# High-part products first, and eight raw buffers for the expert tiles, in a two-layer encoder on one core

## The reference

```python
for i in range(DEPTH):                       # DEPTH = 2
    mod = c_act @ mod_w[i] + mod_b[i]
    sh_a, sc_a, g_a, sh_f, sc_f, g_f = jnp.split(mod, N_MOD, axis=-1)
    y = mixers[i % N_MIXERS](modulate(x, norm_g[i, 0], sh_a, sc_a))
    x = x + g_a[:, None, :] * rms_norm(y, norm_g[i, 1])
    y = channel_mixers[i % 2](modulate(x, norm_g[i, 2], sh_f, sc_f))
    x = x + g_f[:, None, :] * rms_norm(y, norm_g[i, 3])
```

```python
for e in range(N_EXPERTS):
    y = y + gates[..., e:e + 1] * swiglu(h, w_gate[e], w_up[e], w_down[e])
```

## Time and profile before

| | |
|---|---|
| median of 3 runs | 1932.63 us (1931.55 to 1934.05) |
| the profiled execution, own time | 1931.99 us |
| its span, first to last instruction | 1930.2 us |
| mean granted TensorE clock | 0.973 |
| busy share of TensorE, VectorE, ScalarE | 89%, 72%, 57% |
| read from HBM | 501.29 MB, 260 GB/s over the span |

### The profile page before, as it was taken

One profiled execution on the slowest core, in us unless ns is written; L12 is line 12 of the kernel. 1 busy time (PEld: TensorE's weight loads), 2 busy tenths in 40 slices (PEclk: granted clock), 3 DMA queues, 4 the chain that ended last, 5 costly groups with the idle time before them and its releaser, 6 DMA issues.

```text
span 1930.2 us, 26016 instructions
## 1 busy us (share of the span) xinstructions
PE 1727.2 (89%) x9941; PEld 1382.1 (72%) x9941; DVE 1380.4 (72%) x1236; ACT 1096.2 (57%) x1075; POOL 51.4 (3%) x100
## 2 busy tenths in 40 slices
PE   1998898899999998889888999899999988999996
PEld 1997898779999686556656676667666656778774
DVE  4557356567677487488687878786878777887885
ACT  2434433543333445477666667676757767767763
POOL 2000000001111000000000000000000000000000
PEclk9998998999999999999999999999999998999998
DMA  9865276138878330289789889898989898989993
GB/s 300 301 238 187 77 252 240 43 128 305 296 273 289 126 131 23 88 300 363 252 285 331 289 303 347 304 348 306 346 300 348 278 317 319 350 328 336 354 343 97
DMA packets 244301, 503.87 MB, mean 261 GB/s; under 512 B 10296, under 2 KB 82144, under 8 KB 244192
## 3 DMA queue, kind: packets, MB, share of 16 engines
q1 hardware_dynamic: 228688, 451.44, 66.3%
q0 software_dynamic: 13824, 50.34, 7.2%
q10 hardware_dynamic: 1680, 0.60, 0.2%
HBM read 501.29 MB, written 1.05 MB: 260 GB/s over the span
## 4 chain that ended last, share of the span: by engine, by line
PE 67%; DVE 15%; ACT 10%; issue 7%; DMA 1%; DVEq 0%; ACTq 0%; POOL 0%; POOLq 0%
PE ps L849 14%; PE ps L850 14%; PE ps L851 14%; DVE wlo L1340 7%; PE ps L1164 7%; ACT whi L544 6%; PE ps L1165 6%; PE ps L1191 4%; PE ps L1146 2%; PE ps L1235 2%; PE ps L901 1%; DMA mraw<-mod_w 1%; DVE acc L1352 1%; ACT arena L744 1%; PE ps L918 1%
## 5 line engine op out<-in xcount | busy, mean ns | idle before, releaser
L1340 DVE TENSOR_TENSOR wlo<-raw,whi 128x2048 fp32r<-128x2048 f32 x428 | 971.8, 2288 | 385.7 <-ACT whi L544 385.2
L544 ACT ACTIVATE whi<-raw 128x2048 fp32r<-128x2048 f32 x428 | 815.3, 1912 | 375.2 <-PE ps L1165 188.2
L1164 PE MATMUL ps<-whi,ahi 128*128 128x512 f32 x560 | 236.0, 421 | 48.8 <-DVE wlo L1340 42.3
L849 PE MATMUL ps<-whi,ahi 128*128 128x512 f32 (+1 forms) x688 | 244.7, 356 | 18.0 <-DVE wlo L1340 14.3
L849 PE MATMUL ps<-ahi,whi 128*128 128x256 f32 x832 | 238.3, 286 | 5.1 <-issue 2.8
L851 PE MATMUL ps<-whi,alo 128*128 128x512 f32 (+1 forms) x688 | 238.8, 347 | 0.0
L850 PE MATMUL ps<-wlo,ahi 128*128 128x512 f32 (+1 forms) x688 | 238.8, 347 | 0.0
L850 PE MATMUL ps<-alo,whi 128*128 128x256 f32 x832 | 237.3, 285 | 0.0
L851 PE MATMUL ps<-ahi,wlo 128*128 128x256 f32 x832 | 237.2, 285 | 0.0
L1165 PE MATMUL ps<-wlo,ahi 128*64 128x512 f32 x560 | 225.0, 402 | 0.0
L1164 PEld LDWEIGHTS ps<-whi,ahi 128*128 128x128 f32 x560 | 108.4, 193 | 115.5 <-issue 69.5
(11 more groups left out here) (229 smaller groups left out, 1985.6 us busy)
## 6 DMA issues: line engine op xcount, KB each, us to landing
raw<-l_exp_w_gate SPq DMA_DIRECT2D x112, 1024.0 KB, 7.0
raw<-l_exp_w_up SPq DMA_DIRECT2D x112, 1024.0 KB, 7.3
raw<-l_exp_w_down SPq DMA_DIRECT2D x112, 1024.0 KB, 6.8
mraw<-mod_w POOLq DMA_DIRECT2D x96, 512.0 KB, 5.7
raw<-l_w_in SPq DMA_DIRECT2D x42, 1024.0 KB, 5.1
raw<-l_ffn_w_gate SPq DMA_DIRECT2D x14, 1024.0 KB, 5.1
raw<-l_ffn_w_up SPq DMA_DIRECT2D x14, 1024.0 KB, 6.2
raw<-l_ffn_w_down SPq DMA_DIRECT2D x14, 1024.0 KB, 5.0
```

The source lines that it names most:

```text
L544: act.activation(whi[s % SPL][:, :], raw[s % RAW][:, :], ACT.Copy).then_inc(hi_done, 1)
L849: pe.matmul(dst, stat[0], mov[0], start=start, stop=False, skip_group_check=True)
L1164: pe.matmul(bank(b), stat, hi, start=start, stop=False, skip_group_check=True)
L1340: dve.tensor_tensor(wlo[s % SPL][:, :], raw[s % RAW][:, :], whi[s % SPL][:, :].bitcast(F32), ALU.subtract).then_inc(lo_done, 1)
```

## The change

The products of an expert tile no longer wait for its low part as a whole. `tile_products` issues all matmuls with the high weights after `hi_done`, the last of them increments a new semaphore `hi_used`; then it waits for `lo_done` and issues those with the low weights, the last of which increments `w_used`. `high(s)` now waits for `hi_used` and `lo_done` of tile `s - 3` in place of `w_used`; `low(s)` still waits for `w_used`. The other users of `products` increment `hi_used` too: their second matmul now is the other high-weight one (the order is kept where the weights are the stationary operand).

The expert tiles up to the M passes go through eight raw buffers in turn, after that through six. The two new buffers take the place of `mraw`, whose four tiles now lie in them, so the first tiles that use them wait for `mod_used`. In a wide step the waits for the copies of gate and up move ahead of all down products, and a wide step's first products wait for an addition of scattered results (`y_add`).

```diff
+RING = 8
+M_LOOP = tile_of(FIRST_M, 0)
+def slot_of(s):
+    if s < M_MOE:
+        return s % RAW
+    if s < M_LOOP:
+        j = (s - M_MOE) % RING
+        return (M_MOE + j) % RAW if j < RAW else j
+    return slot_of(M_LOOP - RING + (s - M_LOOP) % RAW)
...
+def freed_by(s):
+    if M_MOE + RING <= s < M_LOOP:
+        return s - RING + 1
+    return s - RAW + 1
...
+        raw += [sb(f"raw{i}", [P, TILE]) for i in range(RAW, RING)]
-        mraw = [sb(f"mraw{i}", [P, D]) for i in range(MRAW)]
+        mraw = [raw[RAW + i // 2][:, i % 2 * D:i % 2 * D + D] for i in range(MRAW)]
...
-                waits(sp, lo_done, s - RAW + 1 + 6 * rr)
+                if M_MOE + RAW <= s < M_MOE + RING:
+                    sp.wait_ge(mod_used, 12 * KC)
+                else:
+                    waits(sp, lo_done, freed_by(s) + 6 * rr)
...
-                act.wait_ge(landed[s % RAW], 16 * (s // RAW + 1) + 16 * rr)
-                waits(act, w_used, s - SPL + 1 + 6 * rr)
-                act.activation(whi[s % SPL][:, :], raw[s % RAW][:, :], ACT.Copy).then_inc(hi_done, 1)
+                act.wait_ge(landed[slot_of(s)], 16 * uses_of(s) + 16 * rr)
+                waits(act, hi_used, s - SPL + 1 + 6 * rr)
+                waits(act, lo_done, s - SPL + 1 + 6 * rr)
+                act.activation(whi[s % SPL][:, :], raw[slot_of(s)][:, :], ACT.Copy).then_inc(hi_done, 1)
...
-            def products(dst, stat, mov, start, stop):
+            def products(dst, stat, mov, start, stop, last=False, weights_still=False):
                 pe.matmul(dst, stat[0], mov[0], start=start, stop=False, skip_group_check=True)
-                pe.matmul(dst, stat[0], mov[1], start=False, stop=False, skip_group_check=True)
-                return pe.matmul(dst, stat[1], mov[0], start=False, stop=stop, skip_group_check=True)
+                cross = ((stat[1], mov[0]), (stat[0], mov[1]))
+                if weights_still:
+                    cross = cross[::-1]
+                hi = pe.matmul(dst, *cross[0], start=False, stop=False, skip_group_check=True)
+                if last:
+                    hi.then_inc(hi_used, 1)
+                return pe.matmul(dst, *cross[1], start=False, stop=stop, skip_group_check=True)
...
+            def tile_products(s, rr, high, low):
+                pe.wait_ge(hi_done, s + 1 + 6 * rr)
+                for dst, stat, a, start in high:
+                    ins = pe.matmul(dst, stat, whi[s % SPL][:, a:a + BANK], start=start, stop=False, skip_group_check=True)
+                ins.then_inc(hi_used, 1)
+                ready(s, rr)
+                for dst, stat, a, stop in low:
+                    ins = pe.matmul(dst, stat, wlo[s % SPL][:, a:a + BANK], start=False, stop=stop, skip_group_check=True)
+                ins.then_inc(w_used, 1)
...
+                    high, low = [], []
+                    for kk in range(4):
+                        kc, a = 4 * k + kk, kk * BANK
+                        first, last = kc == 0, kc == KC - 1
+                        if has_a(PASSES[q]):
+                            high += [(bank(ba), ahi[:, kc, 0:P], a, first), (bank(ba), alo[:, kc, 0:P], a, False)]
+                            low += [(bank(ba), ahi[:, kc, 0:P], a, last)]
+                        if has_b(PASSES[q]):
+                            high += [(bank(bb), tail_of(q)[:, kc, :], a, first)]
+                            low += [(half_bank(bb), tail_of(q)[:, kc, 0:HP], a, last)]
+                    tile_products(s + k, rr, high, low)
...
+                if wide:
+                    pe.wait_ge(gb_copied, steps_b(*after) + 1)
+                    pe.wait_ge(ub_copied, steps_b(*after) + 1)
...
-                if has_a(kind):
+                if q == WIDE:
                     waits(pe, yb_add, added)
+                    pe.wait_ge(y_add, 1 + 4 * ((i + 1) // 2))
```

More of the change, by code:

```diff
@@ L120, in tile_of, with uses_of @@
     return M_MOE + max(6 * n - 2, 0)
+RING = 8
[7 more added lines that the diff above has]
+    return slot_of(M_LOOP - RING + (s - M_LOOP) % RAW)
+def uses_of(s):
+    if s < M_MOE:
+        return s // RAW + 1
+    if s < M_LOOP:
+        first = s - (s - M_MOE) // RING * RING
+        earlier = uses_of(first - RAW) if slot_of(s) < RAW else 0
+        return earlier + (s - M_MOE) // RING + 1
+    return uses_of(M_LOOP - RING + (s - M_LOOP) % RAW) + (s - M_LOOP) // RAW + 1
+def freed_by(s):
+    if M_MOE + RING <= s < M_LOOP:
+        return s - RING + 1
+    return s - RAW + 1
 C_ID, C_ONE, C_UP, C_IOTA, C_DESC, C_EI, C_ORDER, C_SPILL = 0, 128, 256, 384, 512, 520, 528, 536
@@ L288, in build @@
         zeroed = sem("zeroed")
-        landed = [sem(f"landed{i}") for i in range(RAW)]
+        landed = [sem(f"landed{i}") for i in range(RING)]
         hi_done = sem("hi_done")
         lo_done = sem("lo_done")
+        hi_used = sem("hi_used")
         w_used = sem("w_used")
@@ L454, in e_down @@
             def e_down(e, i, s, rr):
-                waits(sp, lo_done, s + 1 - RAW + 1 + 6 * rr)
+                waits(sp, lo_done, freed_by(s + 1) + 6 * rr)
                 for k in (1, 0):
                     src = dram["l1_exp_w_down"][bass.ds(e, 1), bass.ds(i * 512 + 256 * k, 256), :]
-                    sp.dma_start(raw[(s + k) % RAW][:, :].rearrange("p (k n) -> p k n", k=2),
-                                 src.rearrange("a (k p) c -> p (a k) c", p=P)).then_inc(landed[(s + k) % RAW], 16)
+                    sp.dma_start(raw[slot_of(s + k)][:, :].rearrange("p (k n) -> p k n", k=2),
+                                 src.rearrange("a (k p) c -> p (a k) c", p=P)).then_inc(landed[slot_of(s + k)], 16)
             def e_gate(e, i, s, rr):
@@ L528, in fetch_vector @@
                     src = dram["mod_w"][layer, kc * P:(kc + 1) * P, bass.ds(v * D, D)]
-                    pool.dma_start(mraw[kc % MRAW][:, :], src).then_inc(mod_landed[kc % MRAW], 16)
+                    pool.dma_start(mraw[kc % MRAW], src).then_inc(mod_landed[kc % MRAW], 16)
             fetch_vector(0, 0)
@@ L1023, in hidden_T, with down_tile @@
                 ins.then_inc(t_done, 1)
-            def down_tile(f, s, rr, fc0, dense, last=False):
-                if fc0 == 0:
-                    pe.wait_ge(hlo_done, f + 1)
+            def down_tile(f, s, rr, last=False):
+                pe.wait_ge(hlo_done, f + 1)
                 ready(s, rr)
-                for tt in range(NT if dense else 1):
+                for tt in range(NT):
                     for n in range(2):
                         for k in range(2):
-                            fc = (2 * k + tt) if dense else fc0 + k
+                            fc = 2 * k + tt
                             ins = products(bank(2 * tt + n), (hhi[:, fc * P:fc * P + P], hlo[:, fc * P:fc * P + P]),
-                                           weights(s, k * D + n * BANK, k * D + n * BANK + BANK), False, last and k == 1)
-                    if dense and last and tt == 0:
+                                           weights(s, k * D + n * BANK, k * D + n * BANK + BANK), False, last and k == 1,
+                                           tt == NT - 1 and n == 1 and k == 1)
+                    if last and tt == 0:
                         ins.then_inc(first_out, 1)
@@ L1058, in _ @@
             spread_gate(1)
-            down_tile(NHALF - 1, M_IN1 - 1, 0, 0, True, last=True)
+            down_tile(NHALF - 1, M_IN1 - 1, 0, last=True)
             through_boundary(1)
@@ L1160, in tail_of, with half_bank @@
                 return (alo if q == WIDE else ahi)[:, :, P:2 * P]
[L1162 to L1166, removed]
+            def tile_products(s, rr, high, low):
[7 more added lines that the diff above has]
+                ins.then_inc(w_used, 1)
+            def half_bank(b):
+                return ps[0:HP, b * BANK:(b + 1) * BANK]
             def expert_tiles(q, ba, bb, s, rr, between=None):
@@ L1222, in downs @@
-                    ins.then_inc(w_used, 1)
+                    high, low = [], []
+                    for n in range(2):
+                        for kk in range(2):
+                            fc, a = 2 * k + kk, kk * D + n * BANK
+                            first, last = (i == 0 or wide) and fc == 0, (i == NF - 1 or wide) and fc == 3
+                            if has_a(PASSES[q]):
+                                y = bank((4 if wide else 0) + n)
+                                h_hi, h_lo = hhi[:, fc * P:fc * P + P], hlo[:, fc * P:fc * P + P]
+                                high += [(y, h_hi, a, first), (y, h_lo, a, False)]
+                                low += [(y, h_hi, a, last)]
+                            if has_b(PASSES[q]):
+                                b = (2 if wide else 0) + n
+                                high += [(bank(b), hhb[:, fc, :], a, first)]
+                                low += [(half_bank(b), hhb[:, fc, 0:HP], a, last)]
@@ L1339, in low @@
                 waits(dve, w_used, s - SPL + 1 + 6 * rr)
```

(4 more changed lines are left out.)

12 lines of the change are left out of this document (7 added, 5 removed).

## The result

The changed kernel takes 1877.06 us (median of 4 runs, 1873.89 to 1879.56), the kernel before 1933.34 us beside it: a ratio of 0.9696, 95% interval 0.9655 to 0.9736, so 3.0% faster. Forecast were 1893 us and a range of 1870 to 1918. One run of E7 was disturbed (2853.19 us); its ratio and interval leave it out, its median doesn't. The kernel before varies more than the changed one: its median was 1933.34 us here, 1941.27 beside E1 to E4 and 1937.67 beside E5 to E8, so an experiment is compared with the kernel before by its ratio. The profiled execution took 1879.56 us (span 1877.8).

The account below looks back on a forecast made before the run. TensorE led at 89% busy but idled 85.1 us before the M stretch, where VectorE's low set the narrow steps' pace. Terms of 25, 8.5, 3 and 2.5 made 39 us off 1931.99: forecast 1893 us, range 1870 to 1918.

Parts of the forecast that it names:

- more than I count: Rival: stops shrink and TensorE stays at full clock, so all but a third of 90 us returns; 1872 us, chance 0.07.
- 1479.5 to 1644.1: Window with one wide step, then six more steps, two with scatters; 16.3 us idle, of which 8.5 us were to return.
- 829.5 to 940: First expert window, with a 7.16 us stop behind a gather; 2 us there and 1 for the rest, 3 in all.
- (a): High products first in every expert tile: added waits and increments cost nothing; whi freed 0.9 us (narrow) or 1.8 us (wide) earlier.
- the rule's 11 us: Trainium skill's 26.3 ns per matmul increment, an estimated 11 us for 428 new ones, some 1904 us; left out of the sum.
- (b): Step behind a wide step: the 1.2 us stop goes, the 1.03 us stop before wide down products stays; 1.5 us per wide step.
- (c): Narrow steps: whi freed earlier covers VectorE's holes; 3.3 us in a cycle's first run, 2.0 in the second.
- three cycles' worth: 25: Window 940 to 1479.5: 8.3 us per nine-step cycle of 14.3 idle, 25 us over the window.
- The M passes: Last expert stretch, 1644.1 to 1899.6: 4.8 us idle, all at low behind a scatter; 2.5 us gained.
- (d): Eight raw buffers: put at 0, taken as keeping transfers ahead in the narrow run, whose lead would shrink by 4 us.
- (e): Other users of products and the new wait on y_add ahead of a wide step: 0, at worst 1 us in each of seven.
- The signs: Expected marks: 168 us cycle instead of 176.7, narrow steps 14 to 15.9, VectorE's wait for ScalarE from 27.9 to under 15.

Follow-up runs that it names:

- E7: Changed kernel with TensorE again waiting for the low part ahead of a tile and high again waiting for w_used; ratio to the kernel before 1.0003, median 1938.74 us.
- E1: Changed kernel with six raw buffers throughout instead of eight, mraw in tiles of its own; 1877.18 us, ratio to the kernel before 0.9663.
- E4: Changed kernel, but TensorE waits for the low part ahead of a tile's first product; hi_used still frees whi early; 1910.57 us, ratio to the kernel before 0.9843.
- E5: Changed kernel with increments of a semaphore nobody waits for added on expert tiles' high products; 1877.42 us, ratio to the kernel before 0.9685.
- E8: Changed kernel; behind a wide step, the up copy goes ahead of a high and the wide hidden low part ahead of a low; 1873.37 us, ratio to before 0.9665.
- E6: Changed kernel with a wait for lo_done on each low product of an expert tile; 1880.08 us, ratio to the kernel before 0.9700.
- E3: Changed kernel, but high waits for w_used of the tile three back as before; TensorE still starts on high products; 1887.28 us, ratio to the kernel before 0.9723.
- E2: Kernel before with the eight raw buffers alone, products and waits untouched; median 1937.52 us, ratio to the kernel before 0.9986.

## Why the prediction was right, and where its sizes were off

The sign, the mechanism and the place were right: the same matmuls, stops of TensorE removed in the S and L stretch, transfers no obstacle, no price for the split. The size was too small: 54.8 us of the expert part instead of 39. The measured time is inside the stated range, but below my own range of 1880 to 1906, and nearer to the rival "more than I count" (1872, chance 0.07) than to 1893. Term by term the 39 us came out as 34.6 for 25 (940 to 1479.5), 12.6 for 8.5 (1479.5 to 1644.1), 0.7 for 3 (829.5 to 940) and 6.9 for 2.5 (M passes). (The "four stretches" of the prediction's first paragraph are the five whose idle times it lists.) Point by point:

- **(a) no price.** Right. E5 and E6 measured 0.3 ns an increment and at most some 1 ns for a met wait; leaving the rule's 11 us out of the sum was right.
- **(b) behind a wide step.** The stop of 1.17 us ahead of the first narrow tile is gone, as said; what is left of it stands inside the tile, 0.19 us ahead of its low products (at 1309.70). "Stays" was right of the stop ahead of the wide down products, but "I charge nothing" was not: it grew by 0.5 us, and E7 puts 0.7 us a cycle on that edit with its neighbours. A copy that ended 0.12 us too late (1343.14 against 1343.02) before was the warning, and with everything else moved forward it became the last to arrive.
- **(c) the narrow run.** The five steps of the first half gave 5.7 us by the windows (4.8 forecast), the three narrow steps of the second 2.7 (3.5 forecast, 26.4 and 23.8 apart): together 8.4 against 8.3. The size was right, the attribution only in part. I had written that `whi` freed 0.9 us earlier covers the holes. Of the cycle's 11.7 us against E7, the split of TensorE's wait gives 9.0 alone (E3, 168.4). Freeing `whi` early gives 3.1 alone (E4, 174.3), an estimated 4.6 at full clock, and 2.7 on top of the split (168.4 to 165.7). The holes show why both are needed. From the end of `low` of tile 260 to the start of `high` of tile 263, which ends the 1.27 us hole, it is 5.1 us before and in E7, 4.1 in E3, 4.2 in E4 and 3.2 in the changed kernel; the hole itself is 0.97 us in E3, 0.98 in E4 and under 0.1 with both. So the split also frees the buffer: when TensorE has the high half behind it as `low` ends, the tile's `w_used` comes 0.9 us sooner by itself.
- **The sum's missing term.** The term that was mis-sized most is "three cycles' worth: 25". It measured 34.6, because the wide step was counted as full and the 2.19 us stop ahead of every second one was left out. I had booked high products that run during `low` at the gather (923.34), and not here. Three such stops are 7.8 us of the 9.6 missing; the first wide step of all, 29.9 us before, came down by 2.5 us too.
- **1479.5 to 1644.1.** 12.6 us instead of 8.5. Part of it is the clock's, granted 0.96 before and 0.98 after. E7, which gains nothing, needs 160.7 us there and E5 150.4, both at 0.99: 10.3 us between them.
- **The M passes.** 6.9 us instead of 2.5. I had taken TensorE's idle time from its busy column, 4.8 us, and that hides a part of each stop, since a matmul counts as busy 0.40 us and the next can start after 0.23. Counted from start to start, what goes beyond 0.23 us sums, scatters left out, to 9.7 us over 33 places before and to 2.7 over 16 after: the difference is the gain. I had said that more than 4 us there would prove me wrong. By that sign the prediction failed here, by the size of a term and not by a price: the stretch is 255.5 us in E7 as before, 249.3 with the split alone (E3) and 252.2 with the early release alone (E4).
- **829.5 to 940.** 0.7 us instead of 3: the clock took the rest, see below.
- **(d) eight buffers at 0.** Right for the gain, wrong as the thing "that lets (c) happen". E1 has all of (c) with six. The run wanted a tile each 2.5 us, as forecast, but the queue rose to 395 GB/s (2.65 us a tile) and six buffers stayed ahead.
- **(e)** The stretch before 829.5 us grew by 2.7 us in this execution, 0.7 in E1, and shrank by 2.6 in E3; its half-clock stretches differ from execution to execution. No run ties anything there to the change.
- **The signs.** I had named a cycle of 168 us (165.7), narrow steps of 14 to 15.9 us (13.9 to 15.2) and VectorE's wait for ScalarE under 15 us per cycle. That wait fell to 17.0 only, and E3 has most of the gain with 26.4: it was a poor sign.

## What to carry to other kernels

Where a product needs a part that is made late, wait for that part at the first product that reads it and put the products that don't in front: it shortens the tail behind the late engine and fills its lateness at once, and here it was worth two to three times what freeing a buffer earlier brought (9.0 us a cycle against 3.1 measured and 4.6 at full clock). The two shorten the same loop, so one alone leaves most of a hole that both together close. Count the stops of a pipelined engine from start to start, each with what ended it, also in steps that look full; the busy column hides up to 0.17 us of each (0.40 us busy, the next start after 0.23). When a change moves everything forward, the waits that were met within some 0.1 us of need are the next ones: look for them in each queue (here a copy behind a `high` and a hidden low part behind a `low`, worth 1.3 us a cycle once both were put first; E8 moves them together).

## What the runs showed of the hardware that was not expected

**TensorE's clock in the head of the expert part.** A stop of 3.6 us ahead of the same tile's products ran on at full clock before and at half clock after. The stop in the kernel before, then in the changed one, where it stands ahead of the low products:

```profile
847.79 0.47 PE L1164 MATMUL ps<-whi,ahi 128*128 128x512 f32 x1 [3.57 <-DVE wlo L1340]
...
849.92 1.97 PE L1215 MATMUL ps<-wlo,ahi 128*64 128x512 f32 x4 [3.55 <-DVE wlo L1390]
```

Windows around it and around the gather that follows, kernel before, then the changed kernel:

```profile
844.00:862.00 18.00, 13.54 (x65) 9.29 (x64) 17.03 (x21) 12.81 (x11) 0.00 (x0) 1.00 0.95 343
...
917.00:940.00 23.00, 15.77 (x64) 10.79 (x64) 16.40 (x13) 18.55 (x18) 0.00 (x0) 0.85 0.72 255
```

```profile
844.00:862.00 18.00, 14.33 (x49) 10.42 (x49) 14.97 (x24) 10.40 (x9) 0.00 (x0) 0.72 1.01 370
918.00:942.00 24.00, 18.95 (x65) 13.67 (x66) 16.39 (x13) 18.88 (x21) 0.00 (x0) 0.72 0.72 244
```

Only the second stop was followed by a stretch at 1.2 GHz (0.72 is the mean of the two levels over the window), and 49 matmuls ran where 65 had; a window 2.3 us later, since the changed kernel's expert part starts later, holds 51. E4, with 0.97 in that stage, needs 106.6 us for it against 109.8:

```profile
829.60:936.20 106.60, 90.02 (x451) 63.93 (x450) 91.56 (x90) 84.34 (x80) 0.00 (x0) 0.97 0.95 352
```

So some 3 us of the gain went to the clock in this stage. The split doesn't decide it: all ten kernels have this stop, 3.54 to 3.58 us long. The clock fell behind it in the changed kernel, in E1, E3, E5, E6 and E8, and also in E7, whose stop stands where it did before; it didn't in the kernel before, E2 and E4. E4 shows that a shorter stop, 2.20 us, can be followed by a fall too. What decides stays open; no run here separates it.

**The transfer queue** moved 395 GB/s over whole steps of 15 us, 385 before. A bound read from the busiest step of a kernel is not the queue's limit.
